# A table of 32 bytes becomes 64, and the four split tiles behind it begin at a multiple of 64 bytes

## The reference

```python
def chunk(xc):                      # PEER, 128 tokens at a time
    ...                             # top 16 x 16 product keys -> 16 experts for each of 8 heads
    idx = e1 * PEER_KEYS + e2       # of 128 * 128 = 16,384 experts
    g = jax.nn.softmax(vs, axis=-1)
    z = jnp.einsum('td,thkd->thk', xc, u_experts[idx])
    a = (jax.nn.gelu(z) * g)        # the gated activations
    return jnp.einsum('thk,thkd->td', a, v_experts[idx])
```

## The kernel before

| tile | begins at byte | past a multiple of 64 | past a multiple of 128 |
|---|---|---|---|
| `u_hi0` (the seven tiles to `v_lo1` follow, 4096 bytes apart) | 157,888 | 0 | 64 |
| `h_hi`, `h_lo` | 190,656 and 198,848 | 0 | 64 |
| `prob_scale` | 223,808 | 0 | 64 |
| `a_hi0` (then `a_hi1`, `a_lo0`, `a_lo1`, 1024 apart), before | 223,840 | 32 | 96 |
| `a_hi0`, after | 223,872 | 0 | 0 |

## Time and profile before

### The profile page before, as it was taken

The page is one execution under the profiler, slowest core; times in us unless marked ns, Lnnn a source line. Parts: engine busy times, 40 slices in busy tenths (PEclk is TensorE's granted clock), DMA queues, the critical chain, the costliest instruction groups (busy, mean ns, idle before and its releaser), DMA issues.

```text
span 1356.1 us, 21959 instructions
## 1 busy us (share of the span) xinstructions
PE 1289.0 (95%) x8283; PEld 1112.7 (82%) x8283; DVE 1064.7 (79%) x2318; ACT 596.8 (44%) x1105; POOL 250.1 (18%) x180
## 2 busy tenths in 40 slices
PE   5889999988999889999999999999999999999997
PEld 5577855685696579999999999999988888888886
DVE  5587896686778689999987888888876666666666
ACT  1444682536334535555544444444443333333332
POOL 0363000550000007689940000000000000000001
PEclk9999999999999999999999999999999999999999
DMA  9877542857577254654454444444565555555552
GB/s 353 299 229 281 210 141 90 300 204 274 186 267 263 94 207 135 202 180 149 152 172 148 141 149 148 148 145 152 171 197 190 187 187 186 187 188 187 188 191 99
DMA packets 92382, 256.82 MB, mean 189 GB/s; under 512 B 9472, under 2 KB 16896, under 8 KB 91904
## 3 DMA queue, kind: packets, MB, share of 16 engines
q1 hardware_dynamic: 59728, 195.91, 43.1%
q10 hardware_dynamic: 32560, 59.66, 12.4%
HBM read 254.47 MB, written 1.06 MB: 188 GB/s over the span
## 4 chain that ended last, share of the span: by engine, by line
PE 60%; DVE 17%; POOL 8%; issue 6%; DMA 5%; ACT 3%; SPq 1%; POOLq 0%; ACTq 0%; DVEq 0%
PE bank L1733 26%; PE bank L1726 21%; PE bank L2005 4%; PE bank L1119 3%; DVE arena L430 2%; PE bank L689 2%; POOL u_lo L1765 2%; DVE arena L966 2%; DMA arena<-in_w_in 2%; POOL v_lo L1765 2%; POOL head_ms L820 2%; DVE u_lo L681 2%; DVE v_lo L681 1%; DMA arena<-in_nsa_w_in 1%; DVE arena L1006 1%
## 5 line engine op out<-in xcount | busy, mean ns | idle before, releaser
L1726 PE MATMUL bank<-h_hi,u_hi 128*128 128x256 f32 x632 | 182.7, 289 | 4.0 <-POOL u_lo L1765 2.9
L1726 PE MATMUL bank<-h_hi,u_lo 128*128 128x256 f32 x632 | 178.7, 283 | 0.0
L1726 PE MATMUL bank<-h_lo,u_hi 128*128 128x256 f32 x632 | 178.7, 283 | 0.0
L1726 PEld LDWEIGHTS bank<-h_hi,u_hi 128*128 128x128 f32 x632 | 121.0, 191 | 4.8 <-POOL u_lo L1765 1.9
L1726 PEld LDWEIGHTS bank<-h_lo,u_hi 128*128 128x128 f32 x632 | 121.1, 192 | 0.0
L2162 POOL TENSOR_SCALAR raw<-raw 128x1024 f32<-128x1024 f32 x1 | 3.0, 2995 | 640.2 <-DMA raw<-in_final_g 640.2
L1726 PEld LDWEIGHTS bank<-h_hi,u_lo 128*128 128x128 f32 x632 | 120.9, 191 | 0.0
L2101 ACT ACTIVATE u_hi<-raw 128x1024 fp32r<-128x1024 f32 x64 | 67.9, 1062 | 109.2 <-PE bank L1733 109.2
L2101 ACT ACTIVATE v_hi<-raw 128x1024 fp32r<-128x1024 f32 x64 | 67.9, 1062 | 106.0 <-PE bank L1733 106.0
L1726 PE MATMUL bank<-h_hi,v_hi 128*128 128x256 f32 x392 | 112.9, 288 | 0.9 <-POOL v_lo L1765 0.9
L1726 PE MATMUL bank<-h_hi,v_lo 128*128 128x256 f32 x392 | 110.8, 283 | 0.0
(11 more groups left out here) (275 smaller groups left out, 3479.7 us busy)
## 6 DMA issues: line engine op xcount, KB each, us to landing
raw<-in_u SPq DMA_DIRECT2D x128, 512.0 KB, 3.5
raw<-in_v SPq DMA_DIRECT2D x128, 512.0 KB, 3.5
arena<-in_ada_t SPq DMA_DIRECT2D x80, 512.0 KB, 5.2
arena<-in_ada_w SPq DMA_DIRECT2D x12, 512.0 KB, 12.1
raw<-in_nsa_w_in ACTq DMA_DIRECT2D x3, 2048.0 KB, 11.7
arena<-in_moba_w_in ACTq DMA_DIRECT2D x3, 2048.0 KB, 13.4
arena<-in_w_in ACTq DMA_DIRECT2D x3, 2048.0 KB, 10.6
arena<-in_w_query ACTq DMA_DIRECT2D x3, 2048.0 KB, 11.5
```

What stands on the lines that cost most here:

```text
L1726: last = pe.matmul(zbank[k].t[:, 0:S], u[:, c, :], h[:, c, :], start=n == 0, stop=n == 3 * DC - 1)
```

## The change

`prob_scale` gets 16 columns in place of 8, 64 bytes in place of 32. Its uses stay. The four tiles `a_hi0` to `a_lo1` behind it begin 32 bytes later. No instruction is added, removed or moved.

```diff
@@ -909,7 +909,7 @@
     nmax = sb("nmax", [P, NT, NH])
     rsum = sb("rsum", [P, NT, NH])
     esink = sb("esink", [P, NT, HA])
-    prob_scale = sb("prob_scale", [P, 8])
+    prob_scale = sb("prob_scale", [P, 16])
     turned_mark, summed_mark = [None] * 5, [None, None]
```

## The result

The changed kernel takes 1353.45 us (median of four runs, 1352.99 to 1353.51), the kernel before 1360.77 us (1357.58 to 1363.65). The ratio is 0.9946, 95% interval 0.9924 to 0.9969: 7.3 us less. It was forecast as 10.4 us less, 1350.8 us.

A forecast was written before the change was run, and what follows sets the result against it. TensorE's unbroken output-product matmuls (L1733) were taken as the bound; 10.4 us less there, every other term nothing, made 1361.2 - 10.4 = 1350.8 us. The forecast's own range was 1348 to 1355 us, the wider one 1344 to 1362.

The forecast's parts named there:

- What bounds the kernel: Output products: TensorE sets the pace, 1500 matmuls of L1733 unbroken in 350.25 us; VectorE and ScalarE wait for it.
- The term of L1733: Output-product matmuls: aligned stationary tiles reach the projection's pace, 0.2335 to 0.2266 us, 10.4 us less over 1503 matmuls.
- the recorded 0.39 us: Sign in the output products: recorded matmuls of `a_hi` with a `hi` part fall from 0.40 to 0.39 us.
- The rule of the Trainium skill: L1733: separate read ports, so the stationary address can't reach the pace; gain 0, 1361 us; chance 0.20 with the order.
- The rival of the order or the bank: Output products: switching bank after every third matmul sets the pace; nothing changes, 1361 us; chance 0.20 with the skill's rule.
- The rival of the uneven rhythm: Output products stay at the projection's slower pace behind a gap, 0.2313 us: 3.3 us less, 1358 us; chance 0.08.
- The slower rival: L1733: streams 64 bytes apart collide more, every distance 0.2375 us, 6.0 us more, 1367 us; chance 0.04 in all.
- The bounds: L1733's gain per matmul: from 0 (alignment doesn't matter) to 0.0202 us (nothing on top of the columns), 30.4 us.
- The covered work: VectorE's splits L1749 and L1751 and ScalarE's work beside the output products: cost nothing; waits shrink by 0.08 us a block.
- The stages ahead: All stages up to 989 us should be as before; if not, the difference isn't this change.

The follow-up runs named there:

- the last kernel: Against the changed kernel, `h` tiles moved by a 48-column table and `prob_scale` given 48 columns, for distances 0 (output products) and 64 (z products): 1344.70 us, ratio to before 0.9870.

## Why the prediction was right in direction, and where its cause and its size were off

- **What bounds the kernel**: right. The chain after has the same piece of 1500 matmuls, and its shortening of 6.65 us came through in full: from the start of the piece to the end of the span it was 363.5 us and is 356.8.
- **The term of L1733** had the wrong cause and, by it, the wrong size. I took the projection's pace for the changed stream, 0.0069 us less for each matmul, 10.4 us; it measured 0.0044 us and 6.65 us (350.25 - 343.60). The row was well read, but its condition was not: the projection has its operands 0 apart, the changed kernel has them 64 short of each other. The step that failed is "the two that agree have both operands at multiples of 64 bytes; ... That's the only place where the tiles of such a stream are off". The distance between the operands was a second difference between the rows, and the last column of the table of places had it. The runs put the distance in the place of the alignment: with all tiles off 64 the gain stays (343.60 us), with the `a` tiles at a multiple of 256 it is gone (350.25 us).
- **Luck.** That the time fell at all, and within the forecast's own 1348 to 1355 us, was luck as far as the cause goes. By the same reasoning a padding of 48 columns would have been forecast at 10.4 us less, and its piece kept 350.25 us. Of the signs that the prediction named, the recorded 0.39 us came; the piece, said to take 339 to 341 us, took 343.60, and the distances didn't become even.
- **The rule of the Trainium skill** that speaks against the change (TensorE: Matmul & The Clock Gate, "Step-by-step: what each phase is for": loading weights doesn't steal read bandwidth from the running matmul) gave a gain of 0. It isn't what these runs show: with the same moving tile and nothing else running, 48 matmuls took 11.22 us or 11.41 us depending only on where the stationary tile lies. So the place of the stationary tile does reach the pace; by which way isn't shown.
- **The rival of the order or the bank** is out: six bare streams in three orders, with and without a bank switch, took 14.05 to 14.06 us, and 343.60 us with the switch taken away.
- **The rival of the uneven rhythm** was nearest in form: the stream did stay uneven, at 0.2291 us, between this rival's 0.2313 and the forecast. It isn't a beginning that doesn't settle, though, but the pace of this distance, to be had again with all tiles moved.
- **The slower rival** looked in the right place (the distance) and was wrong in its price at this point: distance 192 is better than 160. Had the padding been 24 columns or 48, nothing would have been gained (350.25 us), but nothing lost either.
- **The bounds**: 0 and 0.0202 us held. No unbroken stream with 512 columns was under 0.2266 us.
- **The covered work** was costed rightly at nothing: the waits of ScalarE and VectorE shrank by 0.06 us where 0.08 was said, and neither entered the chain.
- **The stages ahead** weren't as before, though the prediction had said so: the profiled execution came 2.7 us later to the piece, 1.7 us of it in a stretch with a clock of 0.86 and 0.9 us by a slower load. The prediction had no term for what differs between executions; the medians hide most of it (7.3 us less against 6.65 in the piece).

## What to carry to other kernels

Where TensorE runs an unbroken stream with a weight load for each matmul, compare the distance from start to start with the same shape elsewhere in the kernel before believing it is at its floor: up to 3% of such a stream (350.25 against 340.28 us) hung here on where two tiles lie to each other. Don't reach for a rounder address. Take the difference of the two starts against 256 bytes, try a handful of paddings, and read the chain's piece, which told 343.60 from 340.28 us with one execution where the whole time of one kernel scatters by up to 7 us. And ask which engine is next: the faster z products of the last kernel ran into VectorE. When a neighbouring stream is used as the yardstick, list every way in which its operands differ, not only the one that the change is about.

## What the runs showed of the hardware that wasn't expected

- The pace of float32r matmuls with a weight load each depends on stationary start minus moving start, against 256 bytes, where all starts are multiples of 32. 512 columns: 0.2269 us at 0, 0.2291 at 192, 0.2325 at 128, 0.2335 at 64, 160 and 224. It is so with the other engines idle too. With both starts 16 past a multiple of 32, distance 0 ran at 0.2335 us.
- For 256 columns the order is different: in bare streams of 96, 10.96 us at 64, 11.44 at 128 and 11.57 at 160. In the kernel, pieces of z products at 64 ran at 0.1135 and at 0.1179 us, so one distance can have more than one pace.
- Alignment to 64 or 256 bytes is worth nothing by itself: 343.60 us with every tile 32 past a multiple of 64, 350.25 us with the stationary tiles at a multiple of 256.
- What in the memory or in TensorE makes the distance count wasn't found, and other types were not tried.
